# Expert weights of a mixture-of-experts stage loaded in chunks of 1 MB instead of 2 MB, in a one-core decoder-layer kernel

## What is computed

```python
def expert_ffn(xb, w_gu, b_gu, w_dn, b_dn):
    gu = xb @ w_gu + b_gu                      # 1024 x 2048
    gate, up = jnp.split(gu, 2, axis=-1)
    gate = jnp.minimum(gate, SWIGLU_LIMIT)
    up = jnp.clip(up, -SWIGLU_LIMIT, SWIGLU_LIMIT)
    glu = gate * jax.nn.sigmoid(SWIGLU_ALPHA * gate)
    return ((up + 1.0) * glu) @ w_dn + b_dn    # 1024 x 1024

# 32 experts, 264 tokens, 4 experts a token:
# h = h + sum over the token's experts of softmax gate * expert_ffn(RMSNorm(h) * norm_moe)
# y = RMSNorm(h) * norm_final
```

## Time and profile before

| What | Value |
|---|---|
| median of three runs | 1424.09 us |
| the profiled execution, and its span | 1423.08 us, 1421.1 us |
| PE busy | 1384.3 us, 97% |
| DVE, ACT, GpSimd busy | 447.7, 219.2, 28.1 us |
| moved by DMA | 494.73 MB, mean 348 GB/s |
| granted TensorE clock, mean | 0.996 |

### The profile page before, as it was taken

The page is one execution under the profiler, slowest core; times in us unless marked ns, Lnnn a source line. Parts: engine busy times, 40 slices in busy tenths (PEclk is TensorE's granted clock), DMA queues, the critical chain, the costliest instruction groups (busy, mean ns, idle before and its releaser), DMA issues.

```text
span 1421.1 us, 16026 instructions
## 1 busy us (share of the span) xinstructions
PE 1384.3 (97%) x6385; PEld 681.5 (48%) x6385; DVE 447.7 (32%) x906; ACT 219.2 (15%) x406; POOL 28.1 (2%) x48
## 2 busy tenths in 40 slices
PE   8999999999999999999999999999999999999997
PEld 6788887677756633333333333333233332333322
DVE  5634344862471421211321312213112121121213
ACT  2220022051123400101101001011010110100102
POOL 0000002200000000000000000000000000000000
PEclk9999999999999999999999999999999999999999
DMA  7643435975379599999999999999999999999995
GB/s 253 203 158 129 148 119 176 349 274 223 119 268 406 218 411 387 429 428 428 428 428 428 428 428 428 429 428 428 428 429 428 429 428 428 429 428 428 428 427 231
DMA packets 69782, 494.73 MB, mean 348 GB/s; under 512 B 8443, under 2 KB 9875, under 8 KB 45149
## 3 DMA queue, kind: packets, MB, share of 16 engines
q1 hardware_dynamic: 64652, 477.55, 81.6%
q0 software_dynamic: 4368, 15.53, 3.0%
q10 hardware_dynamic: 724, 1.11, 0.2%
HBM read 486.12 MB, written 8.22 MB: 348 GB/s over the span
## 4 chain that ended last, share of the span: by engine, by line
PE 81%; DMA 15%; DVE 2%; issue 1%; ACT 1%; ACTq 0%; SPq 0%; DVEq 0%
PE bank L1460 77%; DMA flat<-in_w_gate_up 6%; DMA ring<-in_w_gate_up 6%; PE bank L1471 4%; DMA tokT<-in_w_down 2%; DVE wide L1387 1%; DMA ring<-in_w_in 1%; ACTq L608 0%; ACT wide L605 0%; DVE wide L1392 0%; ACT wide L596 0%; PE bank L1917 0%; DVE wide L1443 0%; ACT L615 0%; ACT L645 0%
## 5 line engine op out<-in xcount | busy, mean ns | idle before, releaser
L1460 PE MATMUL bank<-ring,wide 128*64 128x512 f32 (+2 forms) x1696 | 405.3, 595 | 7.3 <-DMA ring<-in_w_gate_up 6.7
L1460 PE MATMUL bank<-wide 128*64 128x512 f32 (+5 forms) x908 | 272.1, 570 | 11.0 <-DVE wide L1387 7.2
L1460 PE MATMUL bank<-tokT,ring 128*128 128x264 f32 x1152 | 266.0, 389 | 2.2 <-DMA ring<-in_w_in 2.2
L1460 PEld LDWEIGHTS bank<-ring,wide 128*64 128x64 f32 (+2 forms) x1696 | 132.5, 140 | 255.8 <-issue 240.1
L1460 PEld LDWEIGHTS bank<-tokT,ring 128*128 128x128 f32 x1152 | 217.3, 191 | 44.1 <-issue 5.4
L1460 PEld LDWEIGHTS bank<-wide 128*64 128x64 f32 (+3 forms) x908 | 92.3, 155 | 170.2 <-issue 116.4
L596 ACT ACTIVATE wide<-bank 64x512 f32<-64x512 f32 (+3 forms) x105 | 58.8, 561 | 334.5 <-PE bank L1460 212.5
L1411 DVE TENSOR_SCALAR wide<-bank 128x512 f32<-128x512 f32 x32 | 22.1, 692 | 271.3 <-PE bank L1460 271.3
L1460 PE MATMUL bank<-flat,wide 128*64 128x512 f32 (+2 forms) x408 | 92.3, 589 | 3.7 <-DMA flat<-in_w_gate_up 3.7
L1460 PE MATMUL bank<-conv,wide 128*64 128x512 f32 (+1 forms) x400 | 91.1, 596 | 0.3 <-ACT wide L596 0.3
L865 ACT ACTIVATE wide<-wide 128x512 f32<-128x512 f32 x32 | 20.2, 630 | 448.0 <-DVE wide L1411 448.0
(11 more groups left out here) (259 smaller groups left out, 749.3 us busy)
## 6 DMA issues: line engine op xcount, KB each, us to landing
ring<-in_w_gate_up SPq DMA_DIRECT2D x64, 2048.0 KB, 27.1
ring<-in_w_down SPq DMA_DIRECT2D x32, 2048.0 KB, 28.4
flat<-in_w_gate_up SPq DMA_DIRECT2D x16, 2048.0 KB, 27.3
conv<-in_w_gate_up SPq DMA_DIRECT2D x16, 2048.0 KB, 26.3
tokT<-in_w_gate_up SPq DMA_DIRECT2D x16, 2048.0 KB, 27.7
wide<-in_w_gate_up SPq DMA_DIRECT2D x16, 2048.0 KB, 26.8
ring<-in_w_in SPq DMA_DIRECT2D x15, 2048.0 KB, 11.8
wide<-in_w_down SPq DMA_DIRECT2D x8, 2048.0 KB, 25.5
```

The costliest lines, as they stand in the source:

```text
L1460: last[0] = pe.matmul(out, lhsT, rhs, start=start, stop=stop)
```

## The change

The chunks become 1 MB: `wgu` with m=1 and `wdn` with m=2, 8 KB for each partition. A pair has 24 stages, the ring sixteen half slots (both halves of each of the same eight slots), and a refill waits for stage g-15. One more slot of 2 MB (`before_acc`, number 9, outside the ring) holds two chunks of the first pair, so that 20 MB are loaded ahead instead of 18 MB. It lies where `acc` and `ytok` will be, and for that the tokens are kept once: `xtok` holds them unscaled, `select` multiplies `selT` by `rr` instead, the first accumulation reads `xtok` and writes `acc` (`fresh`), and the first scatter takes `b_down` from where it was loaded, with 32 rows of contraction. The gate/up bias of the second expert comes from a second, crossed copy (`bgu_crossed`) in other rows of the array, so that the eight bias matmuls use eight different parts of it. With one gate/up row for a partition the order of the contraction changes: `turn_rows` reads neighbouring columns, `turn_acts` every second. `gmoe` is read from `par`.

```diff
-        RING = [0, 1, 2, 3, 4, 5, 7, 8]
-        FIRST_SLOT = [0, 1, 2, 6, 3, 4, 5, 7, 8, 0, 1, 2]
-        AHEAD = 9
+        RING = [2 * i + y for i in (0, 1, 2, 3, 4, 5, 7, 8) for y in range(2)]
+        FIRST_SLOT = [2 * i + y for i in (0, 1, 2, 6, 3, 9, 4, 5, 7, 8, 0, 1) for y in range(2)]
+        AHEAD = 20
...
-        wgu = a["w_gate_up"][0].rearrange("e (s p m) n -> s e p m n", p=P, m=2)
-        wdn = a["w_down"][0].rearrange("e (s p m) n -> s e p m n", p=P, m=4)
+        wgu = a["w_gate_up"][0].rearrange("e (s p m) n -> s e p m n", p=P, m=1)
+        wdn = a["w_down"][0].rearrange("e (s p m) n -> s e p m n", p=P, m=2)
...
-            for j, name, k in ((2, "so", 1), (4, "so", 1), (5, "so", 3), (0, "so", 3), (1, "xo", 3), (3, "xo", 7)):
+            for j, name, k in ((2, "so", 1), (4, "so", 1), (5, "so", 3), (0, "so", 3), (9, "so", 3), (1, "xo", 3), (3, "xo", 7)):
                 filled(sp, name, k)
-                first_chunk(FIRST_SLOT.index(j))
+                if j == 9:
+                    sp.wait_ge(S["v_out"], 16)
+                first_chunks(j)
...
-            for g, done_stages in zip(range(AHEAD, AHEAD + 8), (1, 2, 3, 5, 6, 7, 8, 9)):
+            for g, done_stages in zip(range(AHEAD, AHEAD + 16), (1, 2, 3, 4, 5, 6, 9, 10, 13, 14, 15, 16, 17, 18, 19, 20)):
                 sp.wait_ge(S["stage_done"], done_stages)
-                refill(g, g // 12)
+                refill(g, g // 24)
             with sp.Fori(0, n * (PAIRS // 2) + (PAIRS // 2 - 1)) as it:
-                for g in range(17, 41):
-                    sp.wait_ge(S["stage_done"], it * 24 + (g - 7))
-                    refill(g, (it * 2 + g // 12) % PAIRS)
+                for g in range(36, 84):
+                    sp.wait_ge(S["stage_done"], it * 48 + (g - 15))
+                    refill(g, (it * 2 + g // 24) % PAIRS)
...
-            for t, n in TILES_P:
-                copy(xtok[0:n, t, :], acc[0:n, t, :], rr[0:n, t:t + 1]).then_inc(S["xtok_ready"], 1)
...
-                ranked(selT, e0).then_inc(S["sel_ready"], 1)
+                st(ranked(selT, e0))
+                v.tensor_tensor(out=selT, in0=selT, in1=bc(rr[:, 0:3], P), op=ALU.mult).then_inc(S["sel_ready"], 1)
...
-                            q = slice(32 * (2 * b + h), 32 * (2 * b + h) + 32)
-                            mm(bank[2 * e + b][64 * h:64 * h + 64, :], onehot[q, 64 * e:64 * e + 64], bgu[q, :], True, False)
+                            rows = 32 * (2 * b + (h ^ e))
+                            mm(bank[2 * e + b][64 * h:64 * h + 64, :], onehot[rows:rows + 32, 64 * e:64 * e + 64],
+                               (bgu, bgu_crossed)[e][rows:rows + 32, :], True, False)
...
-                    w = landed(4 * e + part)
-                    for m in range(2):
-                        k = 2 * part + m
-                        for b in range(2):
-                            for h in range(2):
-                                mm(bank[2 * e + b][64 * h:64 * h + 64, :], xg[:, k, 64 * e:64 * e + 64],
-                                   w[:, m, (2 * b + h) * CW:(2 * b + h + 1) * CW], False, k == KB - 1)
+                    w = landed(8 * e + part)
+                    for b in range(2):
+                        for h in range(2):
+                            mm(bank[2 * e + b][64 * h:64 * h + 64, :], xg[:, part, 64 * e:64 * e + 64],
+                               w[:, 0, (2 * b + h) * CW:(2 * b + h + 1) * CW], False, part == KB - 1)
                     last[0].then_inc(S["stage_done"], 1)
```

More of the change, by code:

```diff
@@ L246, in cut @@
             return moe[:, at[0] - n:at[0]]
-        xtok = cut(3 * D).rearrange("p (t n) -> p t n", t=3)
+        before_acc = moe[:, 0:4 * D]
         acc = cut(3 * D).rearrange("p (t n) -> p t n", t=3)
+        ytok = cut(D)
+        xtok = [cut(D), cut(D)]
+        gts = cut(3 * E).rearrange("p (t n) -> p t n", t=3)
+        zer = cut(E)
+        top = cut(24).rearrange("p (t n) -> p t n", t=3)
+        need = cut(8)
+        rr, rfin = cut(4), cut(4)
+        at[0] = GA * T
         selT = cut(3 * P).rearrange("p (t n) -> p t n", t=3)
@@ L252, in build @@
         xg = cut(KB * P).rearrange("p (k n) -> p k n", k=KB)
+        gT = cut(T)
+        at[0] = SCC * T
+        xtok += [cut(D)]
         mrows, srows = moe[0:11, at[0]:at[0] + 2048], moe[0:10, at[0] + 2048:at[0] + 3072]
@@ L280, in build @@
         slot_full = [sem(f"slot_full{i}") for i in range(6)]
-        moe_full = [sem(f"moe_full{i}") for i in range(9)]
+        moe_full = [sem(f"moe_full{i}") for i in range(20)]
         x_in = [sem(f"x_in{t}") for t in range(3)]
@@ L813, in raw_tokens @@
                 for t, n in TILES_P:
-                    move("xtok", 3 * h + t, acc[0:n, t, 512 * h:512 * h + 512], 512, n)
+                    move("xtok", 3 * h + t, xtok[t][0:n, 512 * h:512 * h + 512], 512, n)
                 if h == 0:
-                    move("xtok", 2, acc[0:TS, 2, 0:512], 512, TS)
+                    move("xtok", 2, xtok[2][0:TS, 0:512], 512, TS)
                 else:
-                    copy(acc[32:32 + TS, 2, 0:512], filled(s, "xtok", 5)[0:TS, 0:512])
+                    done(copy(xtok[2][32:32 + TS, 0:512], filled(s, "xtok", 5)[0:TS, 0:512]), "xtok", 5)
             for k in range(KB):
@@ L830, in _ @@
             s.activation(rr[:, 0:2], b[:, 0:2], ACT.Sqrt, bias=eps[:, 0:1], scale=1.0 / D).then_inc(S["rr_root"], 1)
-            done(s.activation(rr[0:TS, 2:3], b[0:TS, 2:3], ACT.Sqrt, bias=eps[0:TS, 0:1], scale=1.0 / D), "rs")
+            s.activation(rr[0:TS, 2:3], b[0:TS, 2:3], ACT.Sqrt, bias=eps[0:TS, 0:1], scale=1.0 / D)
+            done(s.activation(rr[32:32 + TS, 2:3], b[0:TS, 2:3], ACT.Sqrt, bias=eps[0:TS, 0:1], scale=1.0 / D), "rs")
             raw_tokens(1)
[L833 to L837, removed]
-            for t, n in TILES_P:
-                copy(xtok[0:n, t, :], acc[0:n, t, :], rr[0:n, t:t + 1]).then_inc(S["xtok_ready"], 1)
             for k in range(1, 4):
@@ L897, in _ @@
                 s.wait_ge(S["tile_done"], i + 1)
-                st(s.activation(xtok[0:n, t, :], acc[0:n, t, :], ACT.Square, accum_out=rfin[0:n, t:t + 1]))
+                st(s.activation(xtok[t][0:n, :], acc[0:n, t, :], ACT.Square, accum_out=rfin[0:n, t:t + 1]))
                 s.activation(rfin[0:n, t:t + 1], rfin[0:n, t:t + 1], ACT.Sqrt, bias=eps[0:n, 0:1], scale=1.0 / D)\
@@ L1377, in _, with accumulate @@
             n = v.value_load(npass[0:1, 0:1], min_val=0, max_val=MAXP - 1)
-            v.wait_ge(S["xtok_ready"], 3)
+            emptied(v, "xtok", 5)
             n0, order = st.n, [None, (0, 0), (0, 1), (1, 0), (1, 1)]
-            def accumulate(at, j, last=False):
+            def accumulate(at, j, last=False, fresh=False):
                 v.wait_ge(S["scat_full"], at(5, j + 1))
@@ L1387, in accumulate @@
                         ins = v.tensor_tensor(out=acc[0:TS, 2, 512 * h:512 * h + 512] if last else acc[rows, 2, 0:512],
-                                              in0=bank[6][rows, :], in1=acc[rows, 2, 0:512], op=ALU.add)
+                                              in0=bank[6][rows, :], op=ALU.add,
+                                              in1=xtok[2][rows, 0:512] if fresh else acc[rows, 2, 0:512])
                     return ins.then_inc(S["scat_read"], 1)
@@ L1391, in accumulate, with experts @@
                 dst = acc[:, t, 512 * h:512 * h + 512]
-                return v.tensor_tensor(out=dst, in0=bank[6 + j % 2][:, :], in1=dst, op=ALU.add)\
-                    .then_inc(S["scat_read"], 1)
-            def experts(at, pair, after, final=False):
+                return v.tensor_tensor(out=dst, in0=bank[6 + j % 2][:, :], op=ALU.add,
+                                       in1=xtok[t][:, 512 * h:512 * h + 512] if fresh else dst).then_inc(S["scat_read"], 1)
+            def experts(at, pair, after, final=False, fresh=False):
                 if not final:
@@ L2035, in down @@
                     pe.wait_ge(S["actT_ready"], at(2, e + 1))
-                    for part in range(2):
-                        w = landed(8 + 2 * e + part)
-                        for m in range(4):
+                    for part in range(4):
+                        w = landed(16 + 4 * e + part)
+                        for m in range(2):
+                            i = 4 * e + 2 * (part % 2) + m
                             for q in range(2):
-                                mm(bank[6 + e][64 * q:64 * q + 64, :], actT[:, 4 * e + m, 64 * part:64 * part + 64],
-                                   w[:, m, q * CW:q * CW + CW], part + m == 0, part == 1 and m == 3)
+                                mm(bank[6 + e][64 * q:64 * q + 64, :], actT[:, i, 64 * (part // 2):64 * (part // 2) + 64],
+                                   w[:, m, q * CW:q * CW + CW], part + m == 0, part == 3 and m == 1)
                         last[0].then_inc(S["stage_done"], 1)
```

131 lines of the change are left out of this document (63 added, 68 removed).

## The result

The changed kernel takes 1433.1 us (median of 4 runs, 1432.93 to 1434.22), the kernel before 1423.5 us beside it: a ratio of 1.0069, with an interval of 1.0056 to 1.0082. It is slower by 9.6 us. The profiled execution took 1433.21 us with a span of 1431.3 us, 10.2 us more than before.

What follows compares the result with a forecast made beforehand. DMA bounds the kernel: an unbroken 428 GB/s stream after the last pause sets the end. Terms -1.74 - 1.74 + 0.16 + 6.9 = +3.6 us gave 1426.7 us on the profiled execution, stated as 1427.2 us; range 1419 to 1434 us.

Steps and rivals of the forecast that it cites:

- the forecast: Whole kernel: slower by the sum of all terms, 1427.2 us, own range 1424 to 1430 us; chance 0.58.
- the second rival: Weight stream: packets cost twice as much, +13.3 us for them, +10.0 us in sum, 1433.6 us; chance 0.14.
- What bounds the kernel: Weight stream: DMA full at 428 GB/s; last pause's end, bytes left over the rate and last chunk's matmuls set the end.
- Smaller packets: Weight chunks in 8 KB instead of 16 KB packets: 0.039 us more for each 2 MB, times 176, +6.9 us.
- The three windows inside the cache loads: Attention cache transfers with 4 KB runs: 422, 418 and 409 GB/s against 428; 418 taken to price a packet.
- Earlier refills: Last pause before 538 us: its refill waits for half a stage's work, so the uninterrupted stream starts 1.74 us earlier.
- Start of the first pair: Before and in PE's first pair: second selection pass costs 0.56 us, bias eight abreast saves 0.4 us; together +0.16 us.
- The last chunk: End of the run: PE has 8 instructions instead of 16 behind the last landing, -1.74 us.
- 20 MB ahead: Pause from 463 us: the added 2 MB fill 4.9 us of it but lengthen a later pause; counted as nothing.
- No cost of a DMA as such: Weight transfers: a cost of each DMA besides its packets cannot be told apart and got no term.

Runs made afterwards that it cites:

- the last experiment: Kernel before with first pair's first down projection ahead of the gather, last chunk in four 512 KB DMAs, gate/up bias on eight parts: 1420.0 us, 0.997.
- the late load: Changed kernel with the two chunks in slot 9 issued last of those loaded ahead: 1435.2 us, 1.0079.

## Why the prediction was right, and where its sizes were off

The median, 1433.1 us, lies inside the range, near its upper end, and on the predicted side. It is not the forecast of 1427.2 us, whose own range ended at 1430 us, but close to the second rival's 1433.6 us. That closeness is luck: the rival counts 13.3 us for packets, where 10.9 came, and nothing for the clock, which cost 3.1 us.

*What bounds the kernel.* Right: with the rate at 423 the kernel became slower, though PE's busy time fell, and the bytes behind the last pause over the rate still give the end.

*Smaller packets.* The mechanism was right, the size was not: +6.9 us were counted, +10.9 us came (423 GB/s, where 424 to 425 was to show the forecast), 7.7 ns for each packet more where 4.9 was taken. The three windows inside the cache loads spread from 409 to 422 GB/s; the middle one was chosen, and the run with 4 KB packets shows 410 in a steady stream. The longest window, 10 us, was the right row, and the two of 2 and 3 us were too short to read a rate from. The objection to it, 2 KB runs at its start, did not matter.

*Earlier refills.* Failed, and by an effect that stood in no term: the stage is halved and the refill waits for stage 17, but it came 1.04 us later instead of 1.58 us earlier. The step said that all that moves PE's first pair is the selection and the bias (+0.16 us). The first scatter over 32 rows brought the clock to half for 6.8 us, which cost 0.30 + 2.85 = 3.15 us. Without it the refill would have come at 535.1 us, close to the 535.5 predicted. The runs with 32 and 128 rows show the cause in both kernels.

*Start of the first pair.* The gather began 0.63 us later, where 0.56 was counted. The agreement hides two shifts: PE's instructions up to 476 us stood 0.23 us earlier in this execution, and a wait of 0.27 us for ScalarE, counted nowhere, came in ahead of the transposes at 477.39 us; the selection itself cost 0.59 us. The bias took 1.05 us (492.17 to 493.22) for 1.87: 0.82 us less, near its bound of half, not 0.4. Together -0.2 us for +0.16. That the bias counts in the first pair alone is true of this kernel; in the last experiment, where the pause lies in the second pair, it counts twice.

*The last chunk* was right (-1.72 for -1.74 us). *20 MB ahead* was right: the 2 MB loaded early were missing in the later pause, as the late load shows. *No cost of a DMA as such*: right within what the runs tell, since 24 stages keep 428 GB/s with 16 KB packets, and DMAs of 2 MB, no more in number than before, have 422 with 8 KB packets.

The sum by measured terms: -1.72 for the last chunk, +10.86 for packets, -1.72 for the half stage (538.29 - 536.32 for 537.25 - 533.56), -0.30 for the start, read at the scatter, +3.15 for the clock, -0.09 for shorter transposes; 10.2 us.

## What to carry to other kernels

Where the DMA engines are full to the end, as here, the stream grows in proportion to the number of packets, even from 16 to 8 KB. Finer stages can keep the large packet if two of them share a DMA; here that gave back the loss and gained nothing (1.0007). Read the price of a packet from the longest window that has it. And a finer grain is worth only the part that stands before the last pause and behind the last landing, once each: 1.7 us twice, against a cost on every byte.

## What was not expected of the hardware

**The clock falls under a busy PE.** Six instructions with 32 of 128 rows and 128 columns (after six with 32 rows and 8 columns) were followed by a fall of the granted clock to half, for 3.4 us in the kernel before with these rows and 6.8 us in the changed one, though PE shows 1.00 busy in each whole microsecond of the low clock; with the rows filled up by zeros it stayed at 1.00. But few rows alone do not do it: both gathers of the first pair contract over 8 rows for 4.8 us each, and the clock stays at 1.00 under them and after. In the changed kernel:

```profile
485.00:490.00 5.00, 4.71 (x14) 1.99 (x15) 3.07 (x17) 0.60 (x1) 0.00 (x0) 1.00 1.01 421
530.00:535.00 5.00, 5.00 (x16) 2.05 (x15) 2.67 (x4) 1.23 (x2) 0.00 (x0) 1.00 1.01 413
```

The Trainium skill (TensorE: Matmul & The Clock Gate, section The HAM clock gate) says that the clock goes by how busy PE has been lately. The profile's busy column does not show such a difference here: PE idles for 0.43 us ahead of the fall, and for 0.42 us at the same place in the kernel before, where the clock stays. What else tells the scatter from the gathers stays open.

The clock also fell in some executions and not in others, with 128 rows in use: in three of the twelve profiled runs for 3.4 us between 478 and 482 us, under the transposes from `kept`, and in one for 10 us from 483.9 us on. What decides there stays open too, and each such fall delayed the first gather or its end by about 1 us or more.

**A packet costs 7.7 to 9.4 ns** on one of 16 engines, from three kernels with 8 and 4 KB packets. The Trainium skill (DMA: Bandwidth & Descriptors, section Why small descriptors are slow) has about 3 cycles a packet, by which the stream would be 0.6% longer with 8 KB, an estimate; the trace shows 1.25% (865.57 to 876.43 us), twice as much, and the measurement decides. The same page's section Rules for kernel authors gives at least 1 MiB for each DMA as what maximum bandwidth wants; the run with 8 KB packets in 2 MB DMAs keeps to it and moves 422 for 428 GB/s.
